# Input projections from split halves in three passes, a place of their own for the parked adaLN rows, and interleaved cache positions

## The chip, the core and the metric

The kernel runs on one core of a Trainium2 chip. TensorE (PE) multiplies, ScalarE (ACT) and VectorE (DVE) do the elementwise work, GpSimd (POOL) only issues stores, and SyncE (SP) issues the loads. The metric is the device time of one execution in microseconds (us); lower is better.

## The reference, cut to what matters

One step of a decoder trunk of two layers, for 256 prompt positions and 8 decoded ones, so 264 columns side by side. Each layer normalises `x`, scales and shifts it by adaLN values and sends it through one input projection of 3344 columns, four kinds of head groups, an output projection and a channel mixer (dense in layer 0, eight experts with two chosen in layer 1). The 8 decoded positions also attend to 256 earlier ones, which lie in paged caches.

```python
mod = silu(c) @ w_ada[l] + b_ada[l]                    # adaLN: 6 * 1024 values a row
h = rmsnorm(x, g_mix) * (1 + sc1) + sh1
proj = h @ w_in[l]                                     # 1024 x 3344
y = concat(ssd(proj), fox(proj, past), gated_delta(proj), moba(proj, past))
x = x + gt1 * (y @ w_out[l])
h = rmsnorm(x, g_ffn) * (1 + sc2) + sh2
x = x + gt2 * ffn(h)
```

## The kernel before

Features lie on partitions, the 264 positions in the free dimension. Each engine has one program; they meet at semaphores. `plan_stream` fixes the order in which weights pass through `ring`, four slots of 2 MB each: four adaLN chunks, then per layer nine slabs of `w_in`, the two key caches, the remaining adaLN chunks, the two value caches, two slabs of `w_out`, and in layer 0 the weights of the dense mixer. SP loads a slab (`slab`) as soon as the slab that held its slot before is used up. TensorE counts that in `tile_done`; the last number of each plan entry says how many ticks the entry gives.

**Projection.** `project` makes 26 tiles of 128 output columns, in four runs that the code calls G (8 tiles), S, F and M (6 each). A tile is 8 matmuls in fp32 of 128x128 weights, straight from the slot, on the 264 columns of `hT`; each appears as two instructions of TensorE. Tiles go to banks 0 and 1 in turn. ScalarE drains them (`drain`), VectorE convolves ten of them (`convolve`), ScalarE applies silu (`silus`). Behind S, F and M, `head_norms` needs squares that ScalarE makes from the last drained tiles (lines 1452, 1462, 1468), and then gives square sums, from which ScalarE makes `rstd` by four Ln and four Exp (`head_rms`). Ahead of G, `small` multiplies 16 narrow columns, ScalarE copies the result and `narrow_turn` transposes it.

**adaLN chunks.** A chunk is a slab of `w_ada`. `ada_unit` does one half of its 64 instructions on TensorE; both halves together are called a unit below. ScalarE parks the result in the first 128 columns of the chunk's own slot (`mod_rows`), and TensorE transposes it from there at the next place of the plan (`ada_turn`). Eleven chunks of layer 0 and seven of layer 1 are spread over the stages behind the projection (`gdn`, `chain`, `ssd`, `att0` to `att6`), most of them one chunk a stage; at a stage the turn of the chunk before comes first, then the unit. The key caches hold two of the four slots during this, so the chunks alternate between two.

**Behind the projection.** The delta rule (`gdn_invert`, `gdn_chain`) ends in a small store of its state, `out_gdn_p`; VectorE waits for it (line 1907) before the state-space part (`ssd`) reuses the place. Then come eight steps of attention, with the work of the decoded positions between them, and `decode_attention`, which multiplies the two value caches from the ring (line 1071).

**Dense mixer.** It already works from split halves: ScalarE copies a piece of 1024 weights as fp32r to `w_high`, VectorE subtracts it from the fp32 piece into `w_low`, and `three` gives three matmuls in fp32r for each 128x128 block (high x high, low x high, high x low) on 264 columns.

**Caches.** Each of 16 loads per cache brings one page of 128 KB, 8 KB a partition, to 16 partitions that lie side by side.

Of the kernel before, what the change touches and what calls it, by code (L numbers as in the profile page):

```python
# [30 lines left out]
P = 128  # L31
# [47 lines left out]
def consts():  # L79
# [22 lines left out]
    parts["later"] = (i[:, None] // SC == i[None, :] // SC) & (i[:, None] > i[None, :])  # L102
    parts["own_col"] = (i[:, None] // SC == np.arange(NS)[None, :])
    own_row = np.zeros((P, P))
    own_row[:NS] = (np.arange(NS)[:, None] == i[None, :] // SC)
    parts["own_row"] = own_row
    parts["mates"] = (i[:, None] // SC == i[None, :] // SC)
    slot = np.arange(SP_)[None, :]
    pos = slot // RUN * PAGE + (i[:, None] % SC) * RUN + slot % RUN
# [32 lines left out]
def plan_stream():  # L142

    out = [("ada", 0, (c,), 2) for c in range(MIX_CHUNKS)]
    for l in range(DEPTH):
        if l:
            out += [("ada",) + (NORM_ADA["mix", l][0], (NORM_ADA["mix", l][1],), 2)]
        out += [("in", l, s, s[1] // P) for s in IN_SLABS]
        ada = [("ada", la, (c,), 2) for la, c in MIXER_ADA[l]]
        out += [("k", l, (m,), 0) for m in range(2)] + ada + [("v", l, (m,), 1) for m in range(2)]  # L150
        out += [("out", l, (c,), 4) for c in range(2)]
        if l == 0:
            out += [("ada",) + (NORM_ADA["ffn", l][0], (NORM_ADA["ffn", l][1],), 2)]
            out += [("gu", l, (c,), 4) for c in range(FF // 256)]
            out += [("down", l, (c, h), 4) for c in range(4) for h in range(2)]
# [3 lines left out]
def build(nc, A, O, const_at, NCONST):  # L159
    ctx = ExitStack()  # L160
    with ctx:
        def sb(name, shape, dt=F32):
# [7 lines left out]
                  "hc_copied": "mtok_copied", "hidT_done": "m_turned", "hidT_copied": "dtok_copied",  # L170
                  "yc_ready": "max_ready", "part_done": "den_done", "iota_done": "rden_spread",
# [52 lines left out]
        rounds = sb("rounds", [P, 1], I32)  # L224

        ARENA = 25100

        with nc.sbuf_tensor("arena", [P, ARENA], F32) as arena:
            pass
        PIECE, SPLITS = 1024, 4  # L230
# [56 lines left out]
        phase = top[0]  # L287

# [75 lines left out]
        assert max(end1, end2, top[0] - 2 * SP_ * H) <= ARENA - 2 * SP_ * H, (end1, end2, top[0])  # L364
# [71 lines left out]
        def dense_view(t):  # L436
# [7 lines left out]
            return src, lambda w: w[:, t % SPLITS, 0:nk * P].rearrange("p (k n) -> p k n", k=nk)  # L444

# [65 lines left out]
        def _(sp):  # L511
# [7 lines left out]
            def slab(i):  # L519
# [82 lines left out]
        def _(pe):  # L602
# [42 lines left out]
            def ada_turn(l, c):  # L645
# [3 lines left out]
                rows_ = ring[slot_of[index[("ada", l, c)]]]  # L649
                tick(pe.transpose(b[:, 0:P], rows_[:, 0:P], C("ident")))  # L650
# [67 lines left out]

            def project(l, slabs):
# [379 lines left out]
            def three(out, wh, wl, xh, xl, start, stop):  # L1099
                mm(out, wh, xh, start=start, stop=False)  # L1100
                mm(out, wl, xh, start=False, stop=False)  # L1101
                return mm(out, wh, xl, start=False, stop=stop)  # L1102

# [191 lines left out]
            for l in range(DEPTH):  # L1295
# [45 lines left out]
        def _(act_e):  # L1341
# [15 lines left out]
            def mod_rows(l, c):  # L1357
# [3 lines left out]
                copy(ring[slot_of[i]][:, 0:P], bank[0][:, 0:P], "mod_rows")  # L1361

            def mod_columns(l, c):
                act_e.wait_ge(tile_done, done_at[index[("ada", l, c)]])
# [1119 lines left out]
```

## Time and profile before

| what | value |
|---|---|
| time, median of 3 runs | 1509.15 us (1504.14 to 1519.63) |
| the profiled execution | 1509.24 us, of which the span is 1507.3 us |
| TensorE busy | 1346.8 us, 89% of the span |
| VectorE busy | 882.6 us, 59% |
| ScalarE busy | 642.2 us, 43% |
| mean granted clock of TensorE | 0.916 |

### The profile page before, as it was taken

Reading aid. Unit: us, or ns where it says so; the run is one execution under the profiler, and the core shown is the slowest. Engines: PE = TensorE matmul, PEld = TensorE weight load, DVE = VectorE, ACT = ScalarE, POOL = GpSimd, SP = SyncE. Lnnn points to the kernel's source line nnn. Section 1 sums busy time; section 2 is a strip of 40 time slices with the busy share of each in tenths; the row PEclk is TensorE's granted clock in tenths of the full one; section 3 lists DMA queues with packets and bytes.
Section 4 is the critical chain, followed back from the end, with each engine's and each line's share of the span. In section 5 each row is a group of like instructions: output and inputs, shape, how many; then the busy total and the mean of one; then the engine's idle time right before and its main releaser. Section 6 shows DMA issues by size and latency. Waiting matters only on the chain.

```text
span 1507.3 us, 24422 instructions
## 1 busy us (share of the span) xinstructions
PE 1346.8 (89%) x10071; PEld 1141.2 (76%) x10071; DVE 882.6 (59%) x1575; ACT 642.2 (43%) x1098; POOL 10.1 (1%) x22
## 2 busy tenths in 40 slices
PE   5999888859799998998878877899999999999995
PEld 3887755637799997887756555787978898898875
DVE  1140725541555554131624734799899988988996
ACT  2133212210444432233122201677676767767773
POOL 0000000000000000000000000000000000000000
PEclk9999967759899999999866688999999999999998
DMA  9539245695355354459036482489789889978991
GB/s 390 193 131 127 122 170 192 197 185 238 113 177 197 116 198 147 148 147 185 39 116 208 67 268 101 155 330 354 283 337 355 315 312 330 362 288 331 347 334 65
DMA packets 30327, 326.68 MB, mean 217 GB/s; under 512 B 6019, under 2 KB 6531, under 8 KB 8067
## 3 DMA queue, kind: packets, MB, share of 16 engines
q1 hardware_dynamic: 28738, 319.17, 63.2%
q0 software_dynamic: 1472, 5.89, 1.0%
q8 instruction: 82, 1.34, 0.4%
q14 instruction: 35, 0.28, 0.1%
HBM read 319.15 MB, written 5.89 MB: 216 GB/s over the span
## 4 chain that ended last, share of the span: by engine, by line
PE 78%; DVE 7%; DMA 6%; ACT 4%; issue 3%; SPq 2%; DVEq 0%; POOL 0%; ACTq 0%; POOLq 0%
PE bank L1100 15%; PE bank L1101 14%; PE bank L1102 14%; PE bank L725 12%; PE bank L1096 4%; DMA ring<-in_w_ada 4%; PE bank L767 2%; PE bank L640 2%; DMA ring<-in_cache_moba_v 1%; PE bank L1184 1%; SPq L544 1%; PE bank L617 1%; PE bank L663 1%; DMA out_gdn_p<-arena 1%; PE bank L672 1%
## 5 line engine op out<-in xcount | busy, mean ns | idle before, releaser
L2288 DVE TENSOR_TENSOR w_low<-ring,w_high 128x1024 fp32r<-128x1024 f32 x352 | 399.3, 1171 | 46.1 <-ACT w_high L1668 45.1
L1668 ACT ACTIVATE w_high<-ring 128x1024 fp32r<-128x1024 f32 x352 | 342.2, 1017 | 15.1 <-PE bank L1102 13.9
L725 PE MATMUL bank<-hT,ring 128*128 128x264 f32 x832 | 186.6, 386 | 0.0
L1100 PE MATMUL bank<-w_high,hcH 128*128 128x512 f32 x448 | 184.6, 412 | 2.2 <-DVE w_low L2288 1.8
L725 PEld LDWEIGHTS bank<-hT,ring 128*128 128x128 f32 x832 | 157.7, 190 | 26.9
L1102 PE MATMUL bank<-w_low,hcH 128*128 128x512 f32 x448 | 175.7, 392 | 0.0
L1101 PE MATMUL bank<-w_high,hcL 128*128 128x512 f32 x448 | 175.4, 392 | 0.0
L1346 ACT ACTIVATE arena<-bank 128x264 f32<-128x264 f32 (+8 forms) x128 | 51.7, 409 | 252.9 <-PE bank L725 84.5
L1100 PE MATMUL bank<-w_high,hidH 128*128 128x256 f32 x448 | 128.5, 287 | 3.0 <-DVE w_low L2288 3.0
L1101 PE MATMUL bank<-w_high,hidL 128*128 128x256 f32 x448 | 126.7, 283 | 0.0
L1102 PE MATMUL bank<-w_low,hidH 128*128 128x256 f32 x448 | 126.7, 283 | 0.0
L1100 PEld LDWEIGHTS bank<-w_high,hcH 128*128 128x128 f32 x448 | 84.1, 188 | 37.0 <-DVE w_low L2288 22.6
L1100 PE MATMUL bank<-hH,w_high 128*128 128x264 f32 x352 | 101.0, 287 | 9.2 <-DVE w_low L2164 9.2
L1101 PE MATMUL bank<-hH,w_low 128*128 128x264 f32 x352 | 100.6, 286 | 0.0
L1102 PE MATMUL bank<-hL,w_high 128*128 128x264 f32 x352 | 100.5, 286 | 0.0
L1346 ACT ACTIVATE w_high<-ring 128x1024 fp32r<-128x1024 f32 (+1 forms) x76 | 71.5, 945 | 63.3 <-PE bank L1102 63.3
L1102 PEld LDWEIGHTS bank<-w_low,hcH 128*128 128x128 f32 x448 | 84.1, 188 | 18.5
L2164 DVE TENSOR_TENSOR w_low<-ring,w_high 128x1024 fp32r<-128x1024 f32 (+1 forms) x76 | 80.0, 1080 | 26.3 <-ACT w_high L1346 26.3
L1101 PEld LDWEIGHTS bank<-w_high,hcL 128*128 128x128 f32 x448 | 84.4, 188 | 12.8
L640 PE MATMUL bank<-ring,cT 128*32 128x128 f32 x1536 | 69.9, 357 | 26.4 <-DMA ring<-in_w_ada 26.4
L1100 PEld LDWEIGHTS bank<-w_high,hidH 128*128 128x128 f32 x448 | 85.8, 191 | 3.9 <-issue 3.9
L1101 PEld LDWEIGHTS bank<-w_high,hidL 128*128 128x128 f32 x448 | 85.9, 192 | 0.0
(382 smaller groups left out, 2105.9 us busy)
## 6 DMA issues: line engine op xcount, KB each, us to landing
ring<-in_moe_gu SPq DMA_DIRECT2D x56, 2048.0 KB, 8.2
ring<-in_moe_down SPq DMA_DIRECT2D x32, 1792.0 KB, 7.3
ring<-in_w_ada SPq DMA_DIRECT2D x24, 2048.0 KB, 8.8
ring<-in_w_in SPq DMA_DIRECT2D x16, 1536.0 KB, 6.4
ring<-in_ffn_gu SPq DMA_DIRECT2D x11, 2048.0 KB, 7.9
ring<-in_ffn_down SPq DMA_DIRECT2D x8, 1408.0 KB, 6.0
ring<-in_w_out SPq DMA_DIRECT2D x4, 2048.0 KB, 24.9
ring<-in_cache_fox_k SPq DMA_DIRECT2D x32, 128.0 KB, 7.3
```

The lines of the kernel that those rows point to most:

```text
L544: sp.dma_start(r[b * SC:(b + 1) * SC, g * RUN * GW:(g + 1) * RUN * GW], src[bass.ds(page[b * PAGES + g], 1), :, :].rearrange("o c f -> (o ...
L640: ins = mm(b[j * QUAD:(j + 1) * QUAD, 0:P], cT[:, k, :], w[:, k, j * P:(j + 1) * P], start=k == 0, stop=k == KD - 1)
L725: ins = mm(b[:, 0:NT], w[:, k, m * P:(m + 1) * P], hT[:, k, :], start=k == 0, stop=k == KD - 1)
L767: ins = mm(b[q, h * HD:(h + 1) * HD], lhs(q, g * H + h), rhs(q, g * H + h), start=True, stop=True)
L1096: ins = mm(b[:, 0:NT], w[:, k, m * P:(m + 1) * P], yT[:, k, :], start=k == 0, stop=k == KD - 1)
L1100: mm(out, wh, xh, start=start, stop=False)
L1101: mm(out, wl, xh, start=False, stop=False)
L1102: return mm(out, wh, xl, start=False, stop=stop)
L1346: o.go(A_(out, in_, ACT.Copy), name)
L1668: A_(split(w_high), src, ACT.Copy).then_inc(sem("w_high_ready"), 1)
L2164: v(TT(split(w_low), src, split(w_high), ALU.subtract), "split_low")
L2288: TT(split(w_low), src, split(w_high), ALU.subtract).then_inc(sem("w_low_ready"), 1)
```

## The change

It has three parts. First, `project` works from split halves by `three`: ScalarE copies `hT` to `pH` and each tile's weights to `win_high`, VectorE subtracts to get `pL` and `win_low`; three pairs of buffers are used in turn. `in_high` stands ahead of the drain of the tile three before it, `in_low` stands between the steps of `convolve` and of the norms. Second, parked adaLN rows go to a place `mrow` of their own; the turn no longer ticks, so that an adaLN chunk's slot is free when its unit has ended, and `ada_turn` of layer 1's chunk moves ahead of `small`. Third, cache positions of decoded row b lie on partitions b, b + 8, b + 16 and so on, for keys, values and forget logs, with the masks made to match.

```diff
-    out = [("ada", 0, (c,), 2) for c in range(MIX_CHUNKS)]
+    out = [("ada", 0, (c,), 1) for c in range(MIX_CHUNKS)]
...
+        mrow = sb("mrow", [P, P])
+        PHASE, TILES, IN_SPLITS = 14864, 26, 3
+        with (nc.sbuf_tensor("below_phase", [P, PHASE], F32), nc.sbuf_tensor("pH", [P, KD, NT], F32R) as pH,
+              nc.sbuf_tensor("pL", [P, KD, NT], F32R) as pL,
+              nc.sbuf_tensor("win_high", [P, IN_SPLITS, KD, P], F32R) as win_high,
+              nc.sbuf_tensor("win_low", [P, IN_SPLITS, KD, P], F32R) as win_low):
+            pass
...
+        def in_tile(l, t):
+            s_, m = in_tiles[t]
+            slab = ring[slot_of[index[("in", l) + s_]]]
+            return slab[:, 0:KD * s_[1]].rearrange("p (k n) -> p k n", k=KD)[:, :, m * P:(m + 1) * P]
...
-                            sp.dma_start(r[b * SC:(b + 1) * SC, g * RUN * GW:(g + 1) * RUN * GW],
+                            sp.dma_start(r[b:P:NS, g * RUN * GW:(g + 1) * RUN * GW],
...
-                                load(lf[b * SC:(b + 1) * SC, g * RUN:(g + 1) * RUN, :],
+                                load(lf[b:P:NS, g * RUN:(g + 1) * RUN, :],
...
-                rows_ = ring[slot_of[index[("ada", l, c)]]]
-                tick(pe.transpose(b[:, 0:P], rows_[:, 0:P], C("ident")))
+                pe.transpose(b[:, 0:P], mrow[:, :], C("ident")).then_inc(sem("mod_turned"), 1)
...
             def project(l, slabs):
                 for s in slabs:
-                    w = use(index[("in", l) + s])[:, 0:KD * s[1]].rearrange("p (k n) -> p k n", k=KD)
+                    use(index[("in", l) + s])
                     for m in range(s[1] // P):
+                        t = in_tiles.index((s, m))
+                        o.need("in_w_low", 1 if t else 3)
                         b = fill(tiles[0] % 2, "tile_copied")
+                        wh, wl = win_high[:, t % IN_SPLITS, :, :], win_low[:, t % IN_SPLITS, :, :]
                         for k in range(KD):
-                            ins = mm(b[:, 0:NT], w[:, k, m * P:(m + 1) * P], hT[:, k, :], start=k == 0,
-                                     stop=k == KD - 1)
+                            ins = three(b[:, 0:NT], wh[:, k, :], wl[:, k, :], pH[:, k, :], pL[:, k, :], k == 0,
+                                        k == KD - 1)
                         tick(ins)
...
-                small(l)
                 if l:
                     ada_turn(*NORM_ADA["mix", l])
-                else:
+                small(l)
+                if l == 0:
                     pe.wait_ge(sem("start_landed"), 16)
...
-                copy(ring[slot_of[i]][:, 0:P], bank[0][:, 0:P], "mod_rows")
+                copy(mrow[:, :], bank[0][:, 0:P], "mod_rows")
...
+            def in_high(l, t):
+                s_, m = in_tiles[t]
+                i = index[("in", l) + s_]
+                if m == 0:
+                    act_e.wait_ge(landed[slot_of[i]], landed_at[i])
+                if t >= IN_SPLITS:
+                    act_e.wait_ge(tile_done, ticks_before(index[("in", l) + IN_SLABS[0]]) + t + 1 - IN_SPLITS)
+                copy(win_high[:, t % IN_SPLITS, :, :], in_tile(l, t), "in_w_high")
+
             def drain(l, first, n):
                 i0 = ticks_before(index[("in", l) + IN_SLABS[0]])
                 for j in range(first, first + n):
+                    if j + IN_SPLITS < TILES:
+                        in_high(l, j + IN_SPLITS)
                     act_e.wait_ge(tile_done, i0 + j + 1)
...
+                    mod_columns(*NORM_ADA["mix", l])
+                for half in range(2):
+                    act_e.wait_ge(sem("h_ready"), 4 * l + half + 1)
+                    copy(pH[:, 4 * half:4 * half + 4, :], hT[:, 4 * half:4 * half + 4, :], "in_w_high")
+                for t in range(IN_SPLITS):
+                    in_high(l, t)
                 o.need("small_rows")
                 copy(sq[0:16, 3, :], bank[1][0:16, 0:NT], "small_rows_copied")
-                if l:
-                    mod_columns(*NORM_ADA["mix", l])
...
+                for half in range(2):
+                    k = slice(4 * half, 4 * half + 4)
+                    o.need("in_w_high")
+                    v(TT(pL[:, k, :], hT[:, k, :], pH[:, k, :], ALU.subtract), "in_w_low")
+                def in_low(n):
+                    for t in range(split[0], split[0] + n):
+                        o.need("in_w_high")
+                        v(TT(win_low[:, t % IN_SPLITS, :, :], in_tile(l, t), win_high[:, t % IN_SPLITS, :, :],
+                             ALU.subtract), "in_w_low")
+                    split[0] += n
+                in_low(IN_SPLITS)
...
+                in_low(8 - IN_SPLITS)
                 ve.wait_ge(sem("tile_copied"), 26 * l + 6)
                 o.settle()
-                convolve(l, 0, 6, 22, 6, None)
+                convolve(l, 0, 6, 22, 6, None, in_low)
```

`convolve` calls `in_low(1)` ahead of each of its ten channels; `in_low(3)`, `in_low(2)` and `in_low(3)` stand ahead of the norms that follow. Semaphores get second uses, and `consts` and one reduction take the new order of the positions; these have no step of their own below.

## Rows read from the trace of the kernel before

**Rows 1.** The chain that ended last, in order of time: start, duration, what.
```profile
99.97 21.38 PE bank L725 x96
...
201.31 6.51 DMA out_gdn_p<-arena
...
762.52 7.15 DMA out_gdn_p<-arena
```

**Rows 2.** Busy time by stretch: length, each engine (instructions), clock, DMA share, GB/s.
```profile
41.90:70.30 28.40, 28.40 (x130) 24.27 (x129) 5.77 (x21) 3.74 (x16) 0.67 (x1) 1.00 0.40 146
...
389.60:394.00 4.40, 4.35 (x20) 4.38 (x21) 3.31 (x3) 2.36 (x3) 0.00 (x0) 0.50 0.00 0
394.00:584.00 190.00, 189.82 (x1566) 189.61 (x1565) 95.17 (x138) 82.12 (x117) 0.00 (x0) 1.00 0.46 167
...
310.60:318.00 7.40, 4.68 (x16) 3.10 (x16) 2.59 (x9) 3.03 (x8) 0.00 (x0) 0.50 0.97 112
```

**Rows 3.** Groups by line and form: count, busy us, mean ns, idle before.
```profile
L2164 DVE TENSOR_TENSOR w_low<-ring,w_high 128x1024 fp32r<-128x1024 f32 x44 | 51.7, 1217 | 0.0
...
L1346 ACT ACTIVATE w_high<-ring 128x1024 fp32r<-128x1024 f32 x44 | 46.2, 1055 | 26.5 <-PE bank L1102 26.5
...
L1754 DVE SCALAR_TENSOR_TENSOR arena<-arena,cols 128x288 f32<-128x288 f32 x40 | 20.8, 519 | 1.4
```

**Rows 4.** Timeline ahead of layer 1's projection: start, duration, what, idle before.
```profile
594.02 1.94 PE L672 MATMUL bank<-hT,cols 128*16 128x264 f32 x8 [2.27 <-DVE hT L1730]
...
596.60 0.19 DVE L1730 TENSOR_TENSOR hT<-hT,modT 128x32 f32<-128x32 f32 x1
...
598.84 0.38 ACT L1346 ACTIVATE arena<-bank 16x264 f32<-16x264 f32 x1 [6.74 <-PE bank L672]
...
599.84 28.75 PE L725 MATMUL bank<-hT,ring 128*128 128x264 f32 x128
```

**Rows 5.** Timeline of ScalarE in layer 0's projection.
```profile
114.24 0.39 ACT L1346 ACTIVATE arena<-bank 128x264 f32<-128x264 f32 x1 [2.76 <-PE bank L725]
...
117.57 1.36 ACT L1419 ACTIVATE rstd<-rstd 128x264 f32<-128x264 f32 x4
...
121.36 0.39 ACT L1346 ACTIVATE arena<-bank 128x264 f32<-128x264 f32 x1 [2.15 <-PE bank L725]
```

**Rows 6.** Timeline of TensorE in layer 0's projection.
```profile
123.02 2.06 PE L734 MATMUL bank<-arena,cst 128*128 128x264 f32 x8 [1.69 <-ACT arena L1463]
```

**Rows 7.** Timeline of TensorE in layer 0's attention.
```profile
247.19 3.62 PE L640 MATMUL bank<-ring,cT 128*32 128x128 f32 x64 [2.65 <-DMA ring<-in_w_ada]
...
263.84 3.24 PE L640 MATMUL bank<-ring,cT 128*32 128x128 f32 x64 [3.64 <-DMA ring<-in_w_ada]
...
283.83 3.64 PE L640 MATMUL bank<-ring,cT 128*32 128x128 f32 x64
...
333.01 3.38 PE L1071 MATMUL bank<-ring,arena 128*32 128x256 f32 x32 [8.21 <-DMA ring<-in_cache_moba_v]
```

**Rows 8.** The same in layer 1's attention.
```profile
806.14 3.64 PE L640 MATMUL bank<-ring,cT 128*32 128x128 f32 x64 [2.49 <-DMA ring<-in_w_ada]
...
822.46 3.64 PE L640 MATMUL bank<-ring,cT 128*32 128x128 f32 x64 [2.94 <-DMA ring<-in_w_ada]
...
879.70 1.93 PE L1071 MATMUL bank<-ring,arena 128*32 128x256 f32 x32 [0.99 <-DMA ring<-in_cache_moba_v]
```

**Rows 9.** DMA issues: count, KB each, median us from issue to landing.
```profile
ring<-in_w_ada SPq DMA_DIRECT2D x24, 2048.0 KB, 8.8
...
out_gdn_p<-arena POOLq DMA_DIRECT2D x2, 64.0 KB, 6.8
...
out_ssm_p<-arena POOLq DMA_DIRECT2D x2, 64.0 KB, 1.8
```

**Rows 10.** Timeline of TensorE behind layer 0's delta rule: the row products.
```profile
203.31 2.05 PE L716 MATMUL bank<-cst,arena 128*128 128x128 f32 x16
```

**Rows 11.** Timeline of SP: the issue of layer 0's first value cache.
```profile
294.83 8.38 SPq L544 DMA_DIRECT2D ring<-in_cache_fox_v  x16
```

More of the change, by code:

```diff
@@ L101, in consts @@
         parts[f"level{s}"] = (row // (2 * s) == colm // (2 * s)) & (row // s % 2 == 1) & (colm // s % 2 == 0)
-    parts["later"] = (i[:, None] // SC == i[None, :] // SC) & (i[:, None] > i[None, :])
-    parts["own_col"] = (i[:, None] // SC == np.arange(NS)[None, :])
+    parts["later"] = (i[:, None] % NS == i[None, :] % NS) & (i[:, None] > i[None, :])
+    parts["own_col"] = (i[:, None] % NS == np.arange(NS)[None, :])
     own_row = np.zeros((P, P))
-    own_row[:NS] = (np.arange(NS)[:, None] == i[None, :] // SC)
+    own_row[:NS] = (np.arange(NS)[:, None] == i[None, :] % NS)
     parts["own_row"] = own_row
-    parts["mates"] = (i[:, None] // SC == i[None, :] // SC)
+    parts["mates"] = (i[:, None] % NS == i[None, :] % NS)
     slot = np.arange(SP_)[None, :]
-    pos = slot // RUN * PAGE + (i[:, None] % SC) * RUN + slot % RUN
+    pos = slot // RUN * PAGE + (i[:, None] // NS) * RUN + slot % RUN
     sl = 2.0 ** (-8.0 * (np.arange(H) + 1) / H)
@@ L142, in plan_stream @@
 def plan_stream():
-    out = [("ada", 0, (c,), 2) for c in range(MIX_CHUNKS)]
+    out = [("ada", 0, (c,), 1) for c in range(MIX_CHUNKS)]
     for l in range(DEPTH):
         if l:
-            out += [("ada",) + (NORM_ADA["mix", l][0], (NORM_ADA["mix", l][1],), 2)]
+            out += [("ada",) + (NORM_ADA["mix", l][0], (NORM_ADA["mix", l][1],), 1)]
         out += [("in", l, s, s[1] // P) for s in IN_SLABS]
-        ada = [("ada", la, (c,), 2) for la, c in MIXER_ADA[l]]
+        ada = [("ada", la, (c,), 1) for la, c in MIXER_ADA[l]]
         out += [("k", l, (m,), 0) for m in range(2)] + ada + [("v", l, (m,), 1) for m in range(2)]
@@ L152, in plan_stream @@
         if l == 0:
-            out += [("ada",) + (NORM_ADA["ffn", l][0], (NORM_ADA["ffn", l][1],), 2)]
+            out += [("ada",) + (NORM_ADA["ffn", l][0], (NORM_ADA["ffn", l][1],), 1)]
             out += [("gu", l, (c,), 4) for c in range(FF // 256)]
@@ L224, in build @@
         rounds = sb("rounds", [P, 1], I32)
-        ARENA = 25100
+        mrow = sb("mrow", [P, P])
+        ARENA = 25360
         with nc.sbuf_tensor("arena", [P, ARENA], F32) as arena:
             pass
+        PHASE, TILES, IN_SPLITS = 14864, 26, 3
[4 more added lines that the diff above has]
+            pass
+        end0 = PHASE + 2 * KD * NT + 2 * IN_SPLITS * KD * P
+        in_tiles = [(s_, m) for s_ in IN_SLABS for m in range(s_[1] // P)]
+        assert len(in_tiles) == TILES
         PIECE, SPLITS = 1024, 4
@@ L287, in build @@
         phase = top[0]
+        assert phase == PHASE
         egG = carve((NG * H, CH))
@@ L717, in rows, with three @@
                     ins.then_inc(sem(done), 1)
+            def three(out, wh, wl, xh, xl, start, stop):
+                mm(out, wh, xh, start=start, stop=False)
+                mm(out, wl, xh, start=False, stop=False)
+                return mm(out, wh, xl, start=False, stop=stop)
             def project(l, slabs):
                 for s in slabs:
[L721 removed]
+                    use(index[("in", l) + s])
                     for m in range(s[1] // P):
+                        t = in_tiles.index((s, m))
+                        o.need("in_w_low", 1 if t else 3)
                         b = fill(tiles[0] % 2, "tile_copied")
+                        wh, wl = win_high[:, t % IN_SPLITS, :, :], win_low[:, t % IN_SPLITS, :, :]
                         for k in range(KD):
[L725 to L726 removed]
+                            ins = three(b[:, 0:NT], wh[:, k, :], wl[:, k, :], pH[:, k, :], pL[:, k, :], k == 0,
+                                        k == KD - 1)
                         tick(ins)
@@ L1097, in w_out @@
                         tick(ins)
[L1099 to L1102, printed above, removed]
             def dense():
@@ L1360, in mod_rows @@
                 act_e.wait_ge(tile_done, ticks_before(i) + 1)
-                copy(ring[slot_of[i]][:, 0:P], bank[0][:, 0:P], "mod_rows")
+                copy(mrow[:, :], bank[0][:, 0:P], "mod_rows")
             def mod_columns(l, c):
-                act_e.wait_ge(tile_done, done_at[index[("ada", l, c)]])
+                o.need("mod_turned")
                 copy(modT[:, 4 * c:4 * c + 4, :], bank[1][:, 0:P].rearrange("p (m j) -> p m j", m=4)[:, :, 0:9], "mod_ready")
@@ L1737, in add_bias, with convolve @@
                       prm1[:, 48 * l + lo:48 * l + hi].unsqueeze(2).broadcast_to([P, hi - lo, 9]), ALU.add))
-            def convolve(l, first, n, w0, wn, bias):
+            def convolve(l, first, n, w0, wn, bias, in_low):
                 p0 = 46 * l
@@ L1772, in _ @@
                 modulate(0, prm1[:, 96 + 8 * l:104 + 8 * l])
+                for half in range(2):
+                    k = slice(4 * half, 4 * half + 4)
+                    o.need("in_w_high")
+                    v(TT(pL[:, k, :], hT[:, k, :], pH[:, k, :], ALU.subtract), "in_w_low")
+                split = [0]
+                def in_low(n):
[5 more added lines that the diff above has]
+                in_low(IN_SPLITS)
                 if l == 0:
@@ L1822, in _ @@
                 g_ = [prm2[:, heads + i:heads + i + 1] for i in range(5)]
+                in_low(2)
                 qk_norm((0, 1, 4, 5), (g_[0], g_[0], g_[2], g_[2]), "fm_normed")
+                in_low(3)
+                assert split[0] == TILES
                 qk_norm((2, 3, 6, 7), (g_[1], g_[1], g_[3], g_[3]), "qk_whole")
```

10 lines of the change are left out of this document (7 added, 3 removed).

## The prediction

> **What bounds the kernel now.** I read the page's busy shares first, which stand in the table above: TensorE 89%, VectorE 59%, ScalarE 43%. An average doesn't say what an edit is worth, so the chain of waits in order of time came next: in the projection it holds nothing but line 725, six tiles without a gap in 21.38 us [rows 1], at a granted clock of 1.00, the upper level, with DVE and ACT nearly idle beside them [rows 2]. There a cheaper tile shortens the span by what it saves, as long as the split keeps up. Behind the projection the chain runs through waits: for the store of the delta rule's state, 6.51 and 7.15 us [rows 1], and for adaLN slabs and value caches, whose rows come below. The change touches all three. The sum is made against the profiled execution, 1509.24 us, of which 1507.3 are the span; the median is 1509.15 us. Three runs spread over 1%, so about 1%, 15 us, is what a measurement of this kernel can tell from no change.
>
> **The tile.** Now 21.38 / 6 = 3.56 us [rows 1]. After, a tile is 8 x 3 = 24 matmuls in fp32r with 128x128 weights on 264 columns. The dense mixer runs exactly this shape by the same helper: 1566 starts in 189.82 us at clock 1.00 [rows 2], 0.1212 us each, 24 of them 2.91 us. That saves 0.65 us a tile, and over 52 tiles 33.8 us.
>
> FP8 and Floating Point Precision (TensorE Precision Notes) in the Trainium skill gives true FP32 four passes, by which three would cost three quarters of 3.56, an estimate of 2.67 us a tile. The dense row speaks against it with 2.91; what it would give stands among the rivals.
>
> **The split, and whether it keeps up.** ACT copies 128x1024 weights in 1.055 us, DVE subtracts in 1.217 [rows 3], the same sizes and line forms that the dense mixer uses. With three buffers the copy for tile t + 3 starts when tile t has ended; copy and subtraction take 2.3 us, and it is needed two tiles, 5.8 us, later. ACT per tile: copy 1.06, drain about 0.4, silu some 0.6, together 2.1 of 2.9 us. DVE is tightest beside the convolutions: four steps of at most 0.52 us [rows 3] and a subtraction are 3.3 us, above 2.9. Ten channels stand in two groups of six and four, so the backlog is at most 6 x 0.4 = 2.4 us, and the three buffers give two tiles' time of lead. I take nothing for it; at the other end 10 x 0.4 x 2 layers = 8 us. What is late next is the order on ACT:
>
> - Start. `h_ready` comes at 596.79 in layer 1, the narrow copy begins at 598.84 and the projection at 599.84 [rows 4]. After, the second `pH` copy and three `in_high` stand ahead of the narrow copy: 4 x 1.055 = 4.2, so that copy begins at 601.05, ends at 601.4, and with 0.3 for the turn the first tile starts at 601.75: 1.9 us later. DVE needs two subtractions for `pL` and one for tile 0, ready at 600.6, which is hidden. Behind the waiting ACT stand only softplus and the first drain, needed a tile later. For both layers 3.8 us.
> - S to F. The last drain of S, and so the squares that `head_norms` waits for, now has one `in_high` ahead of it: 1.05 us a layer, 2.1.
> - F to M. Now tile 17's drain starts at 114.24, table load, four Ln and four Exp end at 118.93 [rows 5], 4.7 us, and the last tile ends well after. After, an `in_high` makes it 5.75, while the two tiles left take 5.82. So ACT comes free as F ends and still has two copies and two drains before it, 2.8 us, then the two squares, 1.2: 4.0 us instead of 1.69 [rows 6]. 2.3 a layer, 4.6.
> - M to the end: the last three drains have no copy ahead of them; nothing.
>
> An idle TensorE can lose its clock. After 2.27 us of idle its eight products ran on at the upper level [rows 4]; after 3.64 us, 64 instructions took 3.24, close to the 3.6 of the lower level [rows 7]. The gap of 4.0 us is on that side. The first 20 instructions of the dense mixer, behind a long wait, took 4.35 us at clock 0.50 [rows 2], 2.4 at the other level, so I take 2 us a layer, 4. The gaps of 2.7 and 2.8 us lie between the rows: nothing, or 2 us each.
>
> Projection: 33.8 - 3.8 - 2.1 - 4.6 - 4.0 = 19.3 us.
>
> **The parked rows.** A slot comes free at the end of an adaLN unit, not at the turn a stage later; the 2 MB need 8.8 us from issue to landing [rows 9]. Four waits of TensorE in attention, 2.65, 3.64, 2.49 and 2.94 us [rows 7, 8], together 11.7, should go, since each load leaves one stage earlier. The load that is waited for at 263.84 leaves when the unit at 247.19 ends, which is then 247.19 - 2.65 + 3.62 = 248.2; it lands at 257.0 and is wanted at 263.84 - 3.64 - 2.65 = 257.6. That just fits, and for less lucky ones I leave 0.7 us: 11.0. The lower bound is nothing, where ACT or DVE then ends last; but both were waiting for TensorE's products there.
>
> The same load stands behind the store `out_gdn_p`. It is 64 KB and needs 6.8 us, while `out_ssm_p` of the same size needs 1.8 [rows 9]; it leaves just after the turn that released a 2 MB load, and I take the difference for that load's. Once the slot is free a stage earlier, the store at 201.31 [rows 1] lands at about 203.1. Then ACT's copy of the row products is free to begin when their first half is done, at 204.3 [rows 10], not at 207.8: 3.5 us earlier, and layer 1 has the same pattern. In layer 0 the next slab leaves as those products begin and lands 8.8 us later, at 212.1, for which I take 0.7 off. Together 6.3; if the store is slow by itself, nothing.
>
> **The value caches.** The second value product waits 8.21 us in layer 0 and 0.99 in layer 1 for its cache [rows 7, 8]. The first cache's issue begins at 294.83 [rows 11], since its slot was held to the turn; the unit itself ends at 287.47 [rows 7]. Both caches are 4.2 MB; at the 112 GB/s of the row with a DMA share of 0.97 [rows 2] they need 37.4 us from 287.5, to 324.9, and the second product is wanted at 333.01 - 8.21 = 324.8. So the earlier issue by itself about covers it, and any gain from the interleaving is margin: 9.2 us, at worst 7. SP's queue has `w_out` behind them, which then leaves no later than now. Masks and the strided reduction change no size: nothing.
>
> The 112 GB/s are what SBUF — State Buffer (Door 1) of the Trainium skill expects of 16 neighbouring partitions: they reach 4 of 16 ports, 109 GB/s. Partitions at a step of 8 reach 8 of them, which would bring both caches in an estimated 19 us, long before they are wanted; no row here shows that rate.
>
> **The sum.** 19.3 + 11.0 + 6.3 + 9.2 = 45.8 us; 1509.24 - 45.8 = 1463.4, so 1463 us.
>
> **Rivals.**
> - *The short gaps lose the clock too*, and the backlog of the split shows: 4 gaps x 2 = 8, plus up to 8: 1463 + 8 to 16, about 1472. For it: the gaps come near 2.94, behind which a unit at the lower pace follows [rows 8]. Chance 0.12.
> - *The waits behind the projection only move*: the store is slow by itself (6.3), and ACT or DVE takes the place of the slabs (11.0): 1480. For it: TensorE, DVE and ACT hand over to each other at every step there. Chance 0.12.
> - *Fuller TensorE keeps the upper clock in attention.* Eleven adaLN units lie in the two attentions, and those shown take 3.2 to 3.6 us [rows 7, 8]; where 20 instructions took 4.35 us at 0.50, they take 2.4 at 1.00 [rows 2], so a unit would save some 1.7. If nine units or as much other work ran at the upper level, 15 us go: 1448. If a pass cost a quarter of today's tile, 0.89 us, three would cost 2.67 and save 52 x 0.24 = 12.5 us more: 1451; against it the dense rows [rows 2]. That is the rule of FP8 and Floating Point Precision in the Trainium skill. Chance 0.12 for the two, nearly all of it the first.
> - *The change doesn't do what it says*: the split stalls every tile by as much as the passes save, 33.8 us: 1497, within 1%. Against it: 2.3 us of work for 5.8 of lead. Chance 0.05.
> - *Slower.* If the projection's gaps hold TensorE at the lower level, a tile takes 24 x 0.22 = 5.28 us, 2.37 more than at the upper. With a share x of tiles there the projection changes by 52 x (2.37x - 0.65) plus 10.5 for the gaps, against 26.5 saved behind it; it is over 15 us slower from x = 0.53 on, and at x = 1 the time is 1509 + 89 + 10.5 - 26.5 = 1582. Against it: the dense mixer's stream holds 1.00 for 190 us [rows 2]. Chance 0.03.
>
> **How the numbers follow.** The forecast has 0.56 and its own range of 1455 to 1472 from the bounds of the terms. To leave no more than 2 in 10 out, the range takes in the short gaps, the moved waits and most of the fuller clock: 1447 to 1483. Faster by over 1% (below 1494): the forecast and the first three rivals, 0.92. Within 1%: 0.05. Slower: 0.03.
>
> **What would show it.** Right: tile starts 2.9 us apart at clock 1.00; gaps of 2.7 ahead of F's and 4 us ahead of M's norms; no wait for `in_w_ada` in attention; `out_gdn_p` landing in 2 us; no wait at line 1071. Wrong: TensorE waiting for `win_low` inside a run of tiles, a clock below 0.9 there, or DVE or ACT as the releaser where the slabs were.

## The result and the profile after

The changed kernel takes 0.958 of the time of the kernel before (95% interval 0.950 to 0.966). Two repeats gave 0.9554 (0.951 to 0.960; median 1444.4 us) and 0.9578 (0.955 to 0.961; 1447.3 us). Of the profiled 1509.24 us that is about 1446 us: 63 us gained where the sum had 45.8. One execution of the changed kernel was disturbed (2486 us), so its time is that of its other four (median 1450.9 us), and the rows below are of the first repeat.

The page of the changed kernel, head of it:

```profile
span 1443.8 us, 25416 instructions
...
PE 1295.5 (90%) x10487; PEld 1123.8 (78%) x10487; DVE 948.2 (66%) x1631; ACT 695.7 (48%) x1154; POOL 10.0 (1%) x22
```

Busy time by stretch, after: the first tiles; the tiles behind the gap at 117; and layer 0's and layer 1's work from the norms of M to the first product of `w_out`.

```profile
41.90:70.30 28.40, 26.76 (x219) 25.86 (x218) 18.30 (x34) 14.45 (x29) 0.67 (x1) 1.00 0.44 154
117.40:122.00 4.60, 4.60 (x13) 3.77 (x14) 0.00 (x0) 2.10 (x5) 0.00 (x0) 0.50 0.88 205
141.30:309.20 167.90, 137.26 (x1903) 105.07 (x1903) 94.03 (x260) 43.20 (x124) 2.69 (x5) 0.82 0.58 211
661.70:824.50 162.80, 134.35 (x1643) 102.27 (x1643) 94.23 (x260) 41.65 (x116) 2.69 (x5) 0.76 0.46 168
```

The same two stages in the kernel before:

```profile
148.10:340.00 191.90, 148.21 (x1903) 112.36 (x1903) 94.23 (x260) 43.18 (x124) 2.69 (x5) 0.74 0.58 174
706.10:885.90 179.80, 143.07 (x1643) 108.70 (x1643) 94.36 (x260) 41.32 (x116) 2.69 (x5) 0.72 0.49 135
```

This pair of fences is the main reading. The instructions are the same in number (1903 and 1643), and VectorE and ScalarE are as busy as before. The two stages are 41.0 us shorter (in the second repeat 40.2), and that splits in two: TensorE's idle time falls from 43.7 + 36.7 = 80.4 us to 30.6 + 28.5 = 59.1, by 21.3; and its busy time, for the same work, from 291.3 to 271.6, by 19.7, while its granted clock rises from 0.74 and 0.72 to 0.82 and 0.76. Busy time is modelled, so a second sign: the sixth adaLN unit behind layer 0's projection, at 230.40 below, takes 1.95 us without a wait, where it took 3.62 behind a wait of 2.65 [rows 7]. Not every unit gained; the eighteen of both layers together take 48.4 us where they took 56.5, so 8.1 of the 19.7 us are theirs and the rest is other work.

TensorE in layer 0, after: the last adaLN chunk ahead of the projection, the norms of S, F and M, two units in attention, the value products, and the first products of `w_out`.

```profile
28.68 3.64 PE L658 MATMUL bank<-ring,cT 128*32 128x128 f32 x64 [2.77 <-DMA ring<-in_w_ada]
...
92.74 3.60 PE L759 MATMUL bank<-arena,cst 128*128 128x264 f32 x8 [2.61 <-ACT arena L1487]
...
117.39 3.89 PE L759 MATMUL bank<-arena,cst 128*128 128x264 f32 x8 [3.64 <-ACT arena L1498]
...
141.32 2.05 PE L759 MATMUL bank<-arena,cst 128*128 128x264 f32 x8 [1.69 <-ACT arena L1504]
...
230.40 1.95 PE L658 MATMUL bank<-ring,cT 128*32 128x128 f32 x64
...
238.30 3.64 PE L658 MATMUL bank<-ring,cT 128*32 128x128 f32 x64 [2.44 <-DMA ring<-in_w_ada]
...
299.89 5.72 PE L1096 MATMUL bank<-ring,arena 128*32 128x256 f32 x64 [0.75 <-DVE arena L2169]
...
309.19 28.75 PE L1121 MATMUL bank<-hT,ring 128*128 128x264 f32 x128 [1.77 <-DVE arena L2192]
```

In the kernel before, the norms of S and the first products of `w_out`:

```profile
97.91 2.05 PE L734 MATMUL bank<-arena,cst 128*128 128x264 f32 x8 [1.66 <-ACT arena L1452]
...
339.97 30.14 PE L1096 MATMUL bank<-hT,ring 128*128 128x264 f32 x128 [1.77 <-DVE arena L2137]
```

The gap of 1.66 us behind S is now 2.61, that of 1.69 behind F is 3.64 [rows 6], and that behind M stays 1.69. The wait for a value cache is gone: all 64 instructions run in one piece, where 8.21 us stood between the halves [rows 7]. The four waits for adaLN slabs that the prediction named, 11.7 us, are down to 1.0, but others stand where there was none, as at 238.30, so that the sign of no such wait in attention missed.

DMA issues after, with the median time to landing, against [rows 9]; and VectorE's waits for the store (total, times, longest), 14.5 us before:

```profile
ring<-in_w_ada SPq DMA_DIRECT2D x24, 2048.0 KB, 9.4
ring<-in_w_out SPq DMA_DIRECT2D x4, 2048.0 KB, 7.8
...
ring<-in_cache_moba_v SPq DMA_DIRECT2D x32, 128.0 KB, 2.9
...
out_gdn_p<-arena POOLq DMA_DIRECT2D x2, 64.0 KB, 1.8
```

```profile
DVE arena L1963 <- DMA out_gdn_p<-arena: 4.4, 2, 2.2
```

### The profile page after: what moved, and what is told of

Its sections match the earlier page's. It is cut to its first block, busy times and chain, and to the rows that moved or that the text cites. A ratio compares the mean times of both kernels' runs of the same rounds, so it can differ in the third digit from the quotient of the medians.

```text
span 2484.4 us, 25416 instructions
## 1 busy us (share of the span) xinstructions
PE 2379.0 (96%) x10487; PEld 1937.6 (78%) x10487; DVE 969.7 (39%) x1631; ACT 711.2 (29%) x1154; POOL 10.0 (0%) x22
## 3 DMA queue, kind: packets, MB, share of 16 engines
q0 software_dynamic: 1472, 5.89, 0.6%
## 4 chain that ended last, share of the span: by engine, by line
PE 93%; DVE 3%; issue 2%; ACT 1%; DMA 0%; DVEq 0%; SPq 0%; POOL 0%; POOLq 0%
PE bank L739 22%; PE bank L737 22%; PE bank L738 22%; PE bank L1121 5%; PE bank L658 3%; PE bank L792 2%; PE bank L1204 2%; PE bank L680 1%; PE bank L759 1%; PE bank L635 1%; PE bank L1232 1%; PE bank L689 1%; PE bank L971 1%; PE bank L1244 1%; PE bank L733 1%
## 5 line engine op out<-in xcount | busy, mean ns | idle before, releaser
L737 PE MATMUL bank<-w_high,hcH 128*128 128x512 f32 x448 | 308.0, 687 | 0.0
L739 PE MATMUL bank<-w_low,hcH 128*128 128x512 f32 x448 | 302.5, 675 | 0.0
L738 PE MATMUL bank<-w_high,hcL 128*128 128x512 f32 x448 | 301.7, 673 | 0.0
L737 PE MATMUL bank<-w_high,hidH 128*128 128x256 f32 x448 | 200.1, 447 | 0.0
L737 PE MATMUL bank<-pH,win_high 128*128 128x264 f32 x416 | 187.4, 450 | 0.0
L738 PE MATMUL bank<-pH,win_low 128*128 128x264 f32 x416 | 186.1, 447 | 0.0
L739 PE MATMUL bank<-pL,win_high 128*128 128x264 f32 x416 | 185.6, 446 | 0.0
L739 PEld LDWEIGHTS bank<-w_low,hidH 128*128 128x128 f32 x448 | 155.8, 348 | 0.0
L738 PEld LDWEIGHTS bank<-pH,win_low 128*128 128x128 f32 x416 | 136.9, 329 | 1.0 <-issue 1.0
L739 PEld LDWEIGHTS bank<-pL,win_high 128*128 128x128 f32 x416 | 136.9, 329 | 0.0
```

## The experiments

Three accounts of what was gained beyond the sum were put against each other (17 us by the time above; the expectations say 13, from the first median). Theory 1: TensorE keeps its upper clock in attention, since it waits less. Theory 2: the projection gained more than the sum says. Theory 3: the caches do, through quicker loads. A run's median and ratio to the kernel before stand behind each label; each is compared with runs of the kernel before on its own chip.

**after_again**, the kernel as changed. 

> The changed kernel once more, for an undisturbed profile. Theory 1 (the sum holds part by part, and the 13 us beyond it come from TensorE keeping its upper clock in attention, since the waits there are gone): a span near 1450 us; the projection of layer 0 takes 104.6 - 9.7 = 95 us, tiles 2.9 us apart; TensorE's granted clock in the two attentions, 0.59 to 0.76 before, rises to 0.8 or more. Theory 2 (the projection's gain was sized too small: the gaps and their clock don't cost the 14.5 us put down for them): 87 to 90 us for that projection, and the clock in attention as before. Theory 3 (the caches were sized too small: quicker loads of keys and values free the slots behind them): both of these as in theory 1 and as before, and waits for slabs and caches gone beyond those four and two that were counted.

1444.4 us, 0.9554. Projection of layer 0 from its first tile to M's norms: 96.3 us where it was 106.2; layer 1, 94.9. Theory 2, with its 87 to 90 us, is out. The clock is up in both attentions, though in layer 1 by little.

**only_projection, only_rows, only_interleave**: one part of the change each, with the diff's lines of that part and nothing else. 

> The three-pass projection alone; parked rows and caches as before. Theory 1: 19 us below the kernel before, that is a ratio of 0.987, and the waits for adaLN slabs and value caches stay (11.7 and 9.2 us together). Theory 2: 28 to 33 us below, 0.98. Theory 3: 19 us, 0.987. The rival that the short gaps lose the clock as well: 3 to 11 us.

> The parked rows' own place alone; projection and caches as before, and the turn of layer 1's first chunk stays behind the narrow product. Forecast by the terms: 11.0 for the four waits, 6.3 for the store, 9.2 for the value caches, which the earlier issue alone was to cover: 26.5 us below before, a ratio of 0.982; no wait of TensorE for a value cache. Theory 1: 5 to 13 us more, as the clock holds in attention. Theory 3: 17 us or less, 0.989, since the value caches still come at 112 GB/s and are still waited for. The rival that the waits only move: under 5 us.

> The interleaved positions alone; projection and parked rows as before. By the forecast's terms: the wait of 8.2 and 1.0 us at the value products goes and nothing else does: 9 us below before, 0.994. Theory 1: the same. Theory 3: 15 to 20 us, since keys and forget logs land sooner too and adaLN slabs behind them in SP's queue with them.

| run | median | ratio (95%) | gain | forecast |
|---|---|---|---|---|
| only_projection | 1492.2 | 0.986 (0.983 to 0.990) | 21 us | 19 |
| only_rows | 1470.3 | 0.973 (0.969 to 0.977) | 41 us | 26.5 |
| only_interleave | 1493.6 | 0.988 (0.985 to 0.992) | 18 us | 9 |

A gain is one less the ratio, times the median of 1510.9 us of the kernel before. The projection is what the sum says. The rows gain 14 us more (theory 1 had 5 to 13), the interleaving 9 us more: 18 us is inside the 15 to 20 of theory 3, which so holds beside theory 1, though not for the rows alone, where it allowed 17. The three add up to 79.5 us, the whole change to 67.4: some 12 us are counted twice, by intervals of 5 to 7 us on either side of each, and 9.2 of them must be, since either of the last two takes away the wait for value caches.

The rows alone, same two stages:

```profile
150.60:320.00 169.40, 139.60 (x1902) 105.90 (x1903) 94.09 (x260) 43.32 (x124) 2.69 (x5) 0.80 0.65 193
684.90:846.10 161.20, 134.42 (x1642) 103.75 (x1642) 93.91 (x260) 41.35 (x116) 2.69 (x5) 0.76 0.55 166
```

Idle time here falls by 80.4 - 56.6 = 23.8 us, near the forecast's 26.5, which was a sum of waits. Busy time falls by another 17.3, which no term had.

**before_fillers**: is it the clock? In the kernel before, TensorE works through the waits, on useless products called fillers below, instead of standing still; the adaLN slabs, the turns and the caches are as before.

```diff
+            def spin(out, n):
+                for _ in range(n):
+                    mm(out, C("ones"), C("ident"), start=True, stop=True)
...
+                b = fill(0, "mod_rows") if half == 0 else bank[0]
+                spin(b[:, 0:P], spins)
                 if half == 0:
                     use(index[("ada", l, c)])
-                b = fill(0, "mod_rows") if half == 0 else bank[0]
```

> The kernel before with useless products of 128x128 (ones times identity) on TensorE while it waits for an adaLN slab (six of the waits, four to seven products each) or for a value cache (sixteen and two): every wait stays as long as it is, only TensorE is not idle in it. Theory 1 (the clock): the units behind such a wait take 2 us instead of 3.6, and the kernel is 5 to 12 us faster than before, 0.992 to 0.997. Theory 3 and the sum (only the length of the waits counts): the same as before, or up to 4 us slower where the products overrun a wait.

1497.8 us, 0.9932 (0.990 to 0.996): 10 us faster, with useless work added and no transfer moved. Three units of its layer 0, the first and the third behind fillers (L635), the second behind a wait without any:

```profile
246.83 1.28 PE L635 MATMUL bank<-cst 128*128 128x128 f32 x10
249.88 1.96 PE L646 MATMUL bank<-ring,cT 128*32 128x128 f32 x64 [1.77 <-DMA ring<-in_w_ada]
...
256.81 3.45 PE L646 MATMUL bank<-ring,cT 128*32 128x128 f32 x64 [1.48 <-DMA ring<-in_w_ada]
...
262.48 1.73 PE L635 MATMUL bank<-cst 128*128 128x128 f32 x14
265.39 1.96 PE L646 MATMUL bank<-ring,cT 128*32 128x128 f32 x64 [1.18 <-DMA ring<-in_w_ada]
```

A wait of 1.2 to 1.8 us is left ahead of each; only what TensorE did ahead of that differs, and the unit takes 1.96 us or 3.45. In the kernel before, the first and the third took 3.62 and 3.24 behind waits of 2.65 and 3.64 [rows 7]. This shows that an idle TensorE costs twice here: the wait, and slower work behind it. TensorE: Matmul & The Clock Gate (HAM oscillation — how this bites in real kernels) in the Trainium skill describes a loop in which each wait for data lets the clock fall and the next block starts slow; these rows agree, 3.45 us against 1.96.

**projection_rows**: all but the interleaving. 

> The changed kernel without the interleaving: projection in three passes and the parked rows' own place, cache positions side by side as before. Forecast (the earlier issue by itself covers the value caches, interleaving is margin): within 3 us of the changed kernel, about 1448 us. Theory 1 (what the sum missed is TensorE's clock, which rises when the waits shorten, whatever transfer they were for): 1448 to 1452 us. Theory 3 (the quicker loads of keys, values and logs are worth something of their own): 8 to 17 us slower than the changed kernel, 1453 to 1462 us, with waits for adaLN slabs behind the key caches.

1457.9 us, 0.965 (0.960 to 0.971), beside 0.9554 (0.951 to 0.960) and 0.9578 (0.955 to 0.961) for the whole change: the interleaving is worth some 11 to 15 us on top, by intervals that touch. The same two stages as in the main reading:

```profile
139.40:315.50 176.10, 144.18 (x1902) 109.50 (x1902) 93.89 (x259) 43.37 (x124) 2.70 (x5) 0.78 0.65 188
669.90:836.00 166.10, 135.86 (x1642) 103.33 (x1642) 94.25 (x259) 41.60 (x116) 2.69 (x5) 0.74 0.57 166
```

They are 11.5 us longer than in the changed kernel, of which 3.1 are idle time and 8.4 busy time. The first adaLN slab behind the key caches:

```profile
151.88 3.61 PE L658 MATMUL bank<-ring,cT 128*32 128x128 f32 x64 [1.17 <-DMA ring<-in_w_ada]
```

In the changed kernel the same unit had no wait. The stretch in which the key caches come in, first this kernel, then the changed one (the last two columns are DMA share and GB/s):

```profile
106.00:128.00 22.00, 18.35 (x122) 17.31 (x121) 9.28 (x14) 15.18 (x29) 0.00 (x0) 0.84 1.03 161
```

```profile
106.00:127.00 21.00, 17.36 (x114) 16.32 (x113) 8.74 (x13) 14.65 (x31) 0.00 (x0) 0.84 0.91 237
```

**after_reordered**: do ScalarE's copies set the gaps? Each drain now stands ahead of the copy, the squares ahead of the last copies, the narrow copy behind the first weight copy.

```diff
-                    if j + IN_SPLITS < TILES:
-                        in_high(l, j + IN_SPLITS)
                     act_e.wait_ge(tile_done, i0 + j + 1)
...
                         copy(fm[:, i, :], b[:, 0:NT], "tile_copied")
+                    if split and j + IN_SPLITS < TILES:
+                        in_high(l, j + IN_SPLITS)
...
-                drain(l, 18, 2)
+                drain(l, 18, 2, False)
...
                 o.go(A_(sq[:, 2:4, :], fm[:, 4:6, :], ACT.Square), "head_squares")
+                for j in (18, 19):
+                    in_high(l, j + IN_SPLITS)
```

> The changed kernel with the same copies in another order on ScalarE: each tile's drain ahead of the copy for the tile three later, the squares of S and F ahead of the last copies, and the narrow copy behind the first weight copy instead of the third. If the gaps are set by these copies, as forecast, the gap ahead of F's norms falls from 2.6 to 1.7 us, that ahead of M's from 3.6 to 1.7, the start comes 1 to 2 us sooner, and TensorE keeps its upper clock behind F, worth 1.3 to 2.7 us a layer: together 5 to 7 us a layer, 10 to 14 us, about 0.992 of the changed kernel. If VectorE or the gap's other steps end last there, under 4 us.

They do: both gaps are short again, and the projection takes 89.1 us in both layers instead of 96.3 and 94.9, with starts 1.5 and 0.8 us sooner: 15.3 us in all, a little over what was expected.

```profile
90.21 2.05 PE L759 MATMUL bank<-arena,cst 128*128 128x264 f32 x8 [1.67 <-ACT arena L1488]
...
111.42 2.05 PE L759 MATMUL bank<-arena,cst 128*128 128x264 f32 x8 [1.76 <-ACT arena L1500]
```

Yet the time is 1441.6 us, 0.9548, no better than the changed kernel. The gain went behind the projection, in the two stages, which are 11.1 us longer in this profile, at an idle time of 58.4 us (59.1 in the changed kernel) and with 11.8 us more of busy time:

```profile
132.60:304.80 172.20, 143.08 (x1902) 109.87 (x1902) 93.88 (x260) 43.05 (x124) 2.69 (x5) 0.78 0.56 208
650.70:820.30 169.60, 140.36 (x1642) 107.35 (x1642) 94.05 (x259) 41.66 (x117) 2.69 (x5) 0.73 0.45 161
```

The first unit there waits and runs at the lower pace; SP's queue says why (start, duration, what):

```profile
145.96 3.34 PE L658 MATMUL bank<-ring,cT 128*32 128x128 f32 x64 [2.11 <-DMA ring<-in_w_ada]
```

```profile
125.30 11.03 SPq L531 DMA_DIRECT2D arena<-in_cache_fox_logf  x16
136.38 111.51 SPq L548 DMA_DIRECT2D ring<-in_w_ada  x11
```

**reordered_logs**: the sixteen small loads of forget logs stand behind the first two adaLN slabs.

```diff
-                    if i == index[("k", l, 1)]:
+                    if i == index[("k", l, 1)] + 2:
                         for b in range(NS):
```

> The reordered kernel with one move more: the sixteen small loads of forget logs stand behind the first two adaLN slabs in SyncE's queue instead of ahead of them. In the reordered kernel the projection was 15 us shorter, yet attention 11 us longer: the first adaLN slab was issued only when the loads of keys and logs had been, at 136.4 us, landed 9.5 us later and was waited for 2.1 and 2.4 us, and the inversion of the delta rule behind it ran at a lower clock. Theory 1 (the queue on SyncE gave the gain back, by that wait and the clock behind it): the wait ahead of the first unit goes in both layers, and the kernel is 6 to 12 us faster than the reordered one, 1430 to 1436 us. The rival (the clock in attention varies from kernel to kernel whatever the wait): the wait goes and the time stays within 3 us of the reordered kernel.

1436.1 us, 0.952 (0.948 to 0.956); the changed kernel on the same chip (**after_pair**: 

> The changed kernel once more, on the same chip as the two above, to compare them with: 1444 us.

) took 1447.3 us, 0.9578. Against the reordered kernel that is 5.5 us by medians and about 4 by the ratios, and those two ran on different chips: short of the 6 to 12 expected, and with intervals that overlap (0.949 to 0.961 before the move). The wait, though, is gone. The slab leaves at 125.86 and its unit waits for nothing:

```profile
144.36 1.96 PE L658 MATMUL bank<-ring,cT 128*32 128x128 f32 x64
```

```profile
125.86 5.96 SPq L548 DMA_DIRECT2D ring<-in_w_ada  x2
132.01 12.35 SPq L531 DMA_DIRECT2D arena<-in_cache_fox_logf  x16
```

```profile
133.10:299.40 166.30, 137.08 (x1902) 105.59 (x1902) 94.07 (x259) 42.98 (x125) 2.70 (x5) 0.82 0.55 202
645.30:802.00 156.70, 127.01 (x1643) 97.64 (x1643) 94.04 (x260) 41.41 (x116) 2.70 (x5) 0.80 0.46 161
```

The two stages are 18.8 us shorter than in the reordered kernel's profile, with the idle time the same (58.9 us) and all of it in busy time (264.1 against 283.4). About half of that is no measure of the move: the profiled execution took 1426.8 us, the least of six with a median of 1436.1, while the one profiled of the reordered kernel, 1442.8, lies near its median of 1441.6. Executions of one kernel differ by 17 to 19 us here, so whether the clock followed this one wait, or varied by itself, is not shown.

**reordered_logs_fillers**: the same with seven and five fillers in two of VectorE's waits (turns of shares 3 and 6). 

> The same with useless products of 128x128 on TensorE in two of the waits left in each layer's attention, those for VectorE's shares (4.1 and 2.9 us; seven and five products). Theory 1 (the clock): the work behind those waits runs at the upper level, 3 to 6 us faster than without the products. If the clock there is held down by the hand-overs between them, the same; if the products overrun the waits, up to 4 us slower.

1428.6 us, 0.946 (0.943 to 0.950): 7.5 us faster than without, by intervals that overlap a little, and 18.7 us, 1.3%, faster than the changed kernel beside it, by intervals well apart. This is the best version here; it leaves out nothing of the computation.

**reordered_logs_flat**: the same as reordered_logs with positions side by side. 

> The kernel with the copies reordered and the forget logs moved back, but cache positions side by side as in the kernel before: what the interleaving is worth once the projection is shorter. Theory 3 (its quicker loads are worth something of their own, as the 13 us between the changed kernel and the one without interleaving said): a wait of 1 us or more at the second value product, the slabs of w_out landing in 15 us or more, and 8 to 15 us slower than with interleaving, 1444 to 1451 us. The rival (those 13 us were the clock's variation between kernels; the waits themselves are worth 2 us): within 4 us of it, 1432 to 1440 us.

1447.0 us, 0.956 (0.951 to 0.960): on the same chip 10.9 us slower than with interleaving by medians, about 6 by the ratios, whose intervals overlap; the 8 to 15 expected are not clearly met. The value wait was only 0.33 us, so that sign missed, while slabs of `w_out` took 17.0 us to land, as expected. What waits is the first slab behind the key caches in layer 0; the loads of the second of these take a median of 14.5 us to land:

```profile
146.65 3.44 PE L658 MATMUL bank<-ring,cT 128*32 128x128 f32 x64 [3.59 <-DMA ring<-in_w_ada]
```

**two_buffers**: the changed kernel with two pairs of split buffers. 

> The changed kernel with two pairs of split buffers instead of three, so that the copy for a tile starts one tile sooner before it is needed: 2.9 us of lead instead of 5.8. Forecast: copy and subtraction take 2.3 us, so tiles without convolutions still follow each other without a gap, while those beside the convolutions (four steps of 0.5 us and a subtraction, 3.3 us a tile on VectorE) and those behind ScalarE's drains stall by 0.5 to 2 us: 10 to 30 us slower than the changed kernel. If the split were late already with three buffers, much more than that; if the lead didn't matter, the same.

1461.1 us, 0.969 (0.964 to 0.974), 1.1 to 1.4% slower than the changed kernel by its two ratios. But the projection is only 1.6 and 2.9 us longer; TensorE's busy time in the two stages behind it is 8.8 us longer at the same idle time. The total fell into the expected range for a reason that was not the expected one: the lead of a single tile is nearly enough, and most of the rest is TensorE's pace.

## Why the prediction was right, and what it missed

The direction held. The range of 1447 to 1483 us held only at its lower end: 1450.9 us in the first runs, 1446 when scaled to the profiled execution, 1444.4 and 1447.3 in the repeats; and it reached so far down only because it took in the third rival. The point of 1463 us was about 17 us too high, and the forecast's own range of 1455 to 1472 missed. By its own terms, from the spans (1507.3 to 1443.8, 63.5 us):

| step | forecast | measured | from |
|---|---|---|---|
| the tile, 52 times 0.65 us | -33.8 | -34.2 | after_reordered, gaps as before: 2 x (106.2 - 89.1) |
| start of the two projections | +3.8 | +3.9 | +3.1 and +0.8 |
| gap behind S | +2.1 | +1.9 | 2 x (2.61 - 1.66) |
| gap behind F | +4.6 | +3.9 | 2 x (3.64 - 1.69) |
| clock behind the gaps | +4.0 | +7.2 | what is left of -21.2 from first tile to M's norms, whatever its cause |
| waits behind the projection | -26.5 | -21.3 | TensorE's idle time |
| pace of the work there | none | -19.7 | TensorE's busy time |
| `w_out` to the first weights of the mixers | none | -5.9 | -3.1 and -2.8 |
| all else | none | +0.7 | the rest of the spans |

The terms that the sum had come to 38.6 us where it had 45.8; 25.6 us came from two that it had not.

**The projection** was right, net 17.3 us where 19.3 were forecast. The 2.91 us of the dense rows [rows 2] hold: 0.66 us a tile were gained. The estimate of 2.67 worked out from FP8 and Floating Point Precision (TensorE Precision Notes) of the Trainium skill was not met: one of the three passes costs 0.97 us a tile, where a quarter of 3.56 is 0.89. The gaps were named for the wrong norms in the last paragraph of the prediction (it is S's and F's norms that wait), but their sizes were within 0.4 us. The start came out right by chance. The new order on ScalarE shows as a wait of 1.64 us ahead of the narrow turn, where it was 0.56: 1.1 us a layer instead of 1.9. In layer 0 the other 2 us come from the adaLN chunks ahead of it: chunk four waits 2.77 us and runs at 3.64 us instead of 0.77 and 1.95. The earlier release of slots is not needed for that: before_fillers, with the release of the kernel before, shows 2.80 and 3.64 us there and starts 2.3 us later, and only_rows starts 2.5 us later with no split at all. In before_fillers and in the changed kernel the sixteen products at 15.7 us took 3.80 us, where they took 6.79, and the second slab of `w_in` left at 22.18 and 21.45 instead of 25.34, earlier into chunk four's load; that it slows that load, and why the products' pace differs, is not shown. Clock behind the gap of F: thirteen instructions in 4.6 us at 0.50, as forecast; in layer 0 some behind S's as well (its norms take 3.60 us instead of 2.05). In layer 1 the first sixteen instructions of the projection also follow each other at 0.22 us instead of 0.12, some 1.6 us behind the start for which the sum had nothing.

**The waits** were nearly right. Those for adaLN slabs fell from 15.6 to 7.1 us, 8.6 where 11.0 were forecast, since some moved to other units; the value caches' 9.2 us went whole; the store lands in 1.8 us as argued, and VectorE's wait for it fell by 10 us, though only 3.5 of the 21.3 us are left for it, where 6.3 were put down. The claim that the earlier issue by itself covers the value caches held to within 0.7 us of wait in only_rows and 1.5 in projection_rows.

**What failed** are two steps. First, "The sum" takes nothing for the pace of the work behind the waits; that was the third rival, fuller TensorE keeping its upper clock, priced at 15 us and given 0.12 together with a dearer pass. It came true beside the forecast: 19.7 us, 8.1 of them in the adaLN units, and before_fillers shows the mechanism by itself. The 5.9 us at `w_out` are the same thing: in layer 0, behind the same wait of 1.77 us, its 128 products take 28.75 us where they took 30.14, and the sixteen behind them 3.80 where they took 5.49. The rows for it stood in the prediction: units of 3.24 to 3.64 us behind waits [rows 7, 8]. Second, "any gain from the interleaving is margin": it is worth 6 to 15 us on top of the other two parts, by projection_rows and reordered_logs_flat. The sum looked at value caches only. The key caches pass through the same queue ahead of the first adaLN slab, whose unit in layer 0 waits 1.17 to 3.59 us without the interleaving and not at all with it in the same order of loads; in layer 1 it waits in neither. Beside projection_rows, 3.1 us of the 11.5 in the two stages are waits and 8.4 the pace of the work.

Not settled: what sets the pace at a given idle time. two_buffers and the changed kernel have the same idle time behind the projection (59.0 and 59.1 us) and busy times of 280.4 and 271.6 (272.9 in the second repeat). All six executions of two_buffers (1457.8 us and up) are slower than the fourteen of the changed kernel behind its three ratios (1456.1 and down), so that difference belongs to the kernel; no run isolates which wait makes it. For the reordered kernels, whose executions spread over 17 to 19 us, a single profile doesn't tell.

## What to carry to other kernels

Price a wait of TensorE at its length plus what the work behind it loses at the lower clock; where short units stand behind waits, that can double the gain of removing them, as here (21.3 us of idle time, 25.6 of pace). Where a wait can't be removed, a few useless products in it are a cheap test of the clock, and here a gain (0.7%, and 0.5% by intervals that overlap). When a stage gets shorter, look at the issuing queue next: sixteen tiny loads ahead of a large one held it up for 11 us, and the reordered projection, 15 us shorter in the profile, brought next to nothing in the time while they stood there. Moving them took the wait away and 4 to 5.5 us of the time, which is within the noise. And see where in the spread of its kernel the profiled execution lies before reading differences between two profiles.

## What was unexpected of the hardware

In the stretch in which the key caches come in, 237 GB/s were moved with interleaved positions and 161 with positions side by side, all loads of the stretch together, with the DMA engines busier in the second (share 0.91 against 1.03); the two caches' loads landed after a median of 4.2 and 3.3 us instead of 9.2 and 17.2 in projection_rows. That agrees in kind with SBUF — State Buffer (Door 1) of the Trainium skill. The estimate of 19 us for two caches, which the prediction worked out from it, was not reached: layer 0's value caches were issued from 266.84 to 288.2 us and landed 2.9 us later, 24 us in all, because each of the 32 issues now takes SyncE some 0.65 us (10.15 us for the first 16, where it was 8.38 [rows 11]). only_interleave takes 10.28 and 10.01 us for them, so it is the interleaving that makes the issues longer. The loads became issue-bound, and the queue behind them longer by 2 to 3.5 us a cache.
